# The S5 recurrence's scans with their powers and products in PSUM banks

## What is computed

```python
def s5_branch(u, A_re, A_im, log_dt, B_re, B_im, C_re, C_im, D, w_glu, b_glu):
    ...
    A_bar = jnp.exp(A * dt)
    B_bar = ((A_bar - 1.0) / A)[..., None] * Bc
    pows = jnp.exp(A[None] * dt[None] * steps)
    ...
    def step(h0, uc):
        bu = jnp.einsum('btgh,gnh->btgn', uc, B_bar)
        a = jnp.broadcast_to(A_bar, bu.shape)
        _, local = lax.associative_scan(combine, (a, bu), axis=1)
        states = local + pows * h0[:, None]
        y = jnp.einsum('btgn,ghn->btgh', states, Cc).real
        return states[:, -1], y
    ...
    y = ys.transpose(1, 0, 2, 3, 4).reshape(b, L, D_S5) + D.astype(f32) * uf
    y = jax.nn.gelu(y)
    y = y * jax.nn.sigmoid(y @ w_glu.astype(f32) + b_glu.astype(f32))
```

## Time and profile before

| | us |
|---|---|
| median of 3 runs | 4154.89 |
| lowest, highest run | 4148.94, 4157.69 |
| profiled execution | 4153.42 |
| its span (first to last instruction) | 4151.6 |
| TensorE busy | 3840.0 |
| VectorE busy | 2210.1 |
| GpSimd busy | 1041.6 |
| ScalarE busy | 902.8 |

### The profile page before, as it was taken

The page is one execution under the profiler, slowest core; times in us unless marked ns, Lnnn a source line. Parts: engine busy times, 40 slices in busy tenths (PEclk is TensorE's granted clock), DMA queues, the critical chain, the costliest instruction groups (busy, mean ns, idle before and its releaser), DMA issues.

```text
span 4151.6 us, 47406 instructions
## 1 busy us (share of the span) xinstructions
PE 3840.0 (92%) x19082; PEld 3102.2 (75%) x19082; DVE 2210.1 (53%) x2823; ACT 902.8 (22%) x1635; POOL 1041.6 (25%) x581
## 2 busy tenths in 40 slices
PE   6999998999999999999989998798999978889998
PEld 5677676788888887888866776577788767778777
DVE  5554557332323266999334523646254994653565
ACT  3434335200000032111010011302111012542131
POOL 1111111344444432333211211131322311003322
PEclk9999999999999999999999998898999986779999
DMA  2000000211212111222211212121553234222111
GB/s 88 21 26 23 29 26 16 71 66 56 66 56 66 63 43 36 87 86 81 71 51 36 71 42 76 44 64 46 138 117 79 81 87 122 62 60 81 61 51 61
DMA packets 139241, 260.25 MB, mean 63 GB/s; under 512 B 45632, under 2 KB 87616, under 8 KB 136000
## 3 DMA queue, kind: packets, MB, share of 16 engines
q1 hardware_dynamic: 72208, 156.26, 13.3%
q10 hardware_dynamic: 66864, 101.63, 7.2%
HBM read 209.35 MB, written 46.14 MB: 62 GB/s over the span
## 4 chain that ended last, share of the span: by engine, by line
PE 82%; DVE 12%; ACT 2%; issue 2%; DMA 1%; SPq 1%; POOL 1%; ACTq 0%; DVEq 0%; POOLq 0%
PE bank L572 22%; PE bank L574 22%; PE bank L573 22%; PE bank L784 2%; PE bank L954 2%; PE bank L821 1%; PE bank L691 1%; PE bank L804 1%; PE bank L943 1%; PE bank L1082 1%; DVE fb L1962 1%; DVE hn L1817 1%; DVE h L2315 1%; DVE xl L1828 1%; DVE ab L1965 1%
## 5 line engine op out<-in xcount | busy, mean ns | idle before, releaser
L572 PE MATMUL bank<-xh,wh 128*128 128x512 f32 x3008 | 1198.0, 398 | 75.1 <-DVE xl L1828 19.2
L573 PE MATMUL bank<-xl,wh 128*128 128x512 f32 x3008 | 1182.2, 393 | 0.0
L574 PE MATMUL bank<-xh,wl 128*128 128x512 f32 x3008 | 1180.9, 393 | 0.0
L529 POOL CAST wh<-raw 128x1024 fp32r<-128x1024 f32 x264 | 282.4, 1070 | 3004.9 <-PE bank L574 2951.3
L572 PEld LDWEIGHTS bank<-xh,wh 128*128 128x128 f32 x3008 | 571.4, 190 | 235.3 <-issue 38.3
L531 POOL TENSOR_TENSOR wl<-raw,wh 128x1024 fp32r<-128x1024 f32 x264 | 673.6, 2552 | 21.1
L574 PEld LDWEIGHTS bank<-xh,wl 128*128 128x128 f32 x3008 | 571.3, 190 | 121.4
L573 PEld LDWEIGHTS bank<-xl,wh 128*128 128x128 f32 x3008 | 572.3, 190 | 114.5
L2109 DVE SCALAR_TENSOR_TENSOR bank<-apad,cols,bank 128x512 f32<-128x512 f32 x406 | 267.9, 747 | 0.0
L1864 DVE TENSOR_TENSOR h<-bank,h 128x512 f32<-128x512 f32 x240 | 165.3, 690 | 153.3 <-PE bank L574 152.4
L1962 DVE TENSOR_TENSOR_SCAN fb<-fb 128x256 f32<-128x256 f32 (+7 forms) x128 | 189.5, 1521 | 73.6 <-ACT ab L1262 73.6
(11 more groups left out here) (340 smaller groups left out, 5408.1 us busy)
## 6 DMA issues: line engine op xcount, KB each, us to landing
raw<-in_wstream SPq DMA_DIRECT2D x264, 512.0 KB, 3.6
spills<-spill ACTq DMA_DIRECT2D x40, 512.0 KB, 2.7
rawm<-in_mod_w ACTq DMA_DIRECT2D x12, 1024.0 KB, 4.9
gate_spill<-gates ACTq DMA_DIRECT2D x16, 512.0 KB, 2.6
tabs<-in_rope ACTq DMA_DIRECT2D x4, 2048.0 KB, 8.5
f<-spills SPq DMA_DIRECT2D x8, 1024.0 KB, 5.7
h<-in_x ACTq DMA_DIRECT2D x4, 1024.0 KB, 11.8
tabs<-gate_spill ACTq DMA_DIRECT2D x4, 1024.0 KB, 7.0
```

Source lines behind the costliest of these rows:

```text
L529: nc.gpsimd.tensor_copy(wh[:, slot], raw[:, slot]).then_inc(S("panel_high"), 1)
L572: nc.tensor.matmul(o, lh, rh, start=start, stop=False)
L573: nc.tensor.matmul(o, lh, rl, start=False, stop=False)
L574: return nc.tensor.matmul(o, ll, rh, start=False, stop=stop)
```

## The change

The bank tensors 2 to 7 are declared after three tensors of two banks each, which are given up at once, so that `scan_a` lies over banks 2 and 3, `scan_t1` over 4 and 5, and `scan_t2` over 6 and 7. Before the first `within_run` one copy puts the powers `s5q` (1024 elements in each partition) into `scan_a`; `within_run` and `next_run` take their factors from there. The two temporaries of `advance` become `scan_t1` and `scan_t2`. So of the two tensors that each of its five operations reads, one lies in PSUM and one in `s5`; the two multiplications also write to PSUM. The order of the instructions is otherwise the same on all engines.

```diff
-        banks = [ctx.enter_context(nc.psum_tensor(f"bank{b}", [P, 512], F32)) for b in range(8)]
+        banks = [ctx.enter_context(nc.psum_tensor(f"bank{b}", [P, 512], F32)) for b in range(2)]
+        with ExitStack() as st:
+            scan_a, scan_t1, scan_t2 = [st.enter_context(nc.psum_tensor(f"scan{n}", [P, 2 * 512], F32)) for n in range(3)]
+        banks += [ctx.enter_context(nc.psum_tensor(f"bank{b}", [P, 512], F32)) for b in range(2, 8)]
...
-                pb_flat = pb[:, :, :, :, :].rearrange("p c q a h -> p (c q a h)")
-                s5t_flat = s5t[:, :, :, :, :].rearrange("p c q a h -> p (c q a h)")
+                powers_a = scan_a[:, :].rearrange("p (c q j) -> p c q j", c=2, q=S5_PAIRS)
 
                 def advance(new, old, a, shape):
                     size = 2 * S5_PAIRS * shape[-1]
                     t1, t2 = [t[:, 0:size].rearrange("p (c q n) -> p c q n", c=2, q=S5_PAIRS)
-                              for t in (pb_flat, s5t_flat)]
+                              for t in (scan_t1, scan_t2)]
                     link(TT(t1, a[0], old, ALU.mult))
                     link(TT(t2, a[1], old, ALU.mult))
...
                 def within_run(j):
                     shape = [P, 2, S5_PAIRS, S5_RUNS]
-                    a = [s5q[:, c, :, 0:1].unsqueeze(1).broadcast_to(shape) for c in range(2)]
+                    a = [powers_a[:, c, :, 0:1].unsqueeze(1).broadcast_to(shape) for c in range(2)]
...
                 def next_run(g):
                     shape = [P, 2, S5_PAIRS, S5_RUN]
-                    a = [s5q[:, c].unsqueeze(1).broadcast_to(shape) for c in range(2)]
+                    a = [powers_a[:, c].unsqueeze(1).broadcast_to(shape) for c in range(2)]
...
                 s5_local(KT - 1)
                 dve.wait_ge(S("s5_stored"), KT)
+                link(V.tensor_copy(powers_a, s5q[:, :, :, :]))
                 for j in range(1, S5_RUN):
                     within_run(j)
```

## The result

| | before | changed |
|---|---|---|
| median, us | 4152.68 (4 runs, 4148.94 to 4157.69) | 4125.02 (4 runs, 4122.91 to 4130.23) |
| profiled execution | 4153.42 | 4130.23 |
| its span | 4151.6 | 4128.2 |

The ratio is 0.9932, with an interval of 0.9916 to 0.9948: 28 us faster, between 22 and 35. A second comparison (experiment 1) gave 0.9936, interval 0.9923 to 0.9949. One of the six executions of the changed kernel there took 12841.23 us; it counts as slow and is left out of the ratio.

The account below looks back on a forecast made before the run. VectorE's queue before s5_outputs(0) was taken as the bound, keeping TensorE waiting. Hold-ups -27.9, copy +1.3 and two meetings +4.6 gave 22.0 us less: 4154.9 - 22.0 = 4132.9 us, range 4126 to 4145.

Parts of the forecast that it names:

- The bound: Before s5_outputs(0): VectorE's queue sets the end of both TensorE waits, 13.22 us for xc and 19.06 us for pb.
- The hold-ups: In the scan, operations beside GpSimd's cast and subtract of ten weight panels lose 27.9 us; a bank operand removes all.
- Own cost of a bank: In the scan's operations, reading or writing PSUM, also strided or over two banks, adds 0 us.
- (b): In the scan's multiplications, the powers' stride in the bank costs 10.3 us, giving 4143.2 us; chance 0.07.
- (d): In the scan, operations reading one bank and writing another, over two banks, run at half rate: 4172 us; chance 0.03.
- The copy: Ahead of the first within_run, copying 1024 elements into a bank adds 1.3 us to VectorE's queue.
- What comes back: Taps of tiles 6 and 7, still in SBUF, now run beside GpSimd's panel work: two meetings, 4.6 us lost.
- The sum: On VectorE's queue, 27.9 - 1.3 - 4.6 = 22.0 us earlier, all reaching the end of the kernel.
- The level and the range: Whole kernel: 4154.9 - 22.0 = 4132.9 us, range 4126 to 4145 with 2 us for scatter on either side.
- rival (a): The scan's strided part gets faster too, up to 21 us on the queue: 4132.3 us; chance 0.80 together with the forecast.
- (c): In the scan, operations with a bank are still held up by GpSimd; only the copy remains, 4156.2 us; chance 0.05.
- (e): The gain is given back after 3352 us, where something comes at its own time: 4150 us or so; chance 0.05.

Follow-up runs that it names:

- experiment 1: The changed kernel, unedited, timed again beside the kernel before: ratio 0.9936 (0.9923 to 0.9949); stretch from the last s5_local to the product's end 124.57 us.
- experiment 3: The changed kernel with only the powers in banks, both temporaries back in SBUF: ratio 0.9975 against the kernel before, stretch 138.48 us.
- experiment 4: The changed kernel with only the temporaries in banks, powers read from SBUF and no copy: ratio 0.9957 against the kernel before, stretch 134.05 us.
- experiment 6: GpSimd's subtract done twice for ten weight panels: ratio 1.0043 in the kernel before, 0.9940 in the changed kernel, both against the kernel before.
- experiment 2: The kernel before, unedited, profiled once more: stretch from the last s5_local to the product's end 149.56 us, rest of the program behind it 795.3 us.
- Experiment 7: The changed kernel with one more copy of the powers between next_run(5) and the taps of tile 7: stretch 126.49 us instead of 124.57, profiled only.
- experiment 8: The changed kernel with four-operation steps, two copies and next_run(4) placed earlier, taps of tiles 6 and 7 adding up in banks: 4122.58 us, ratio 0.9925.

## Why the prediction fell short

Its steps, in its own order:

- **The bound.** Right: TensorE waited for one queue of VectorE; the wait for `xc` went altogether and the second remained, 10.39 us instead of the 13 us forecast.
- **The hold-ups, -27.9 us.** Right as to cause (experiments 3, 4, 6) and nearly as to size. The scan's first part took 3293.30 - 3209.03 = 84.3 us, against 112.9 us before: -28.6 us. The 0.7 us more are small savings in each clean `within_run`, most of them in the strided multiplications: 1.03 us on average instead of 1.05 us. The powers' place alone doesn't explain it, since with one half of the tensors moved, either of them, they take 1.04 us (experiments 3 and 4).
- **Own cost of a bank, 0.** Right, and for the stride in part by luck: 0 had been chosen between a gain of 21 us and a cost of 10.3 us because no row showed the case. It holds for the stride and for the operations over two banks: 1.23 us for 1024 elements before and after. Rivals (b) and (d) fell with it. The 7.1 us that were estimated from the Trainium skill (VectorE: DVE Perf Modes, The TRN2 errata) didn't come; there the measurement decides.
- **The copy, +1.3 us.** Right: 1.22 us and the gap, 1.25 us. The wait for `xc` of tile 6, foreseen as a near miss, was 0.29 us.
- **What comes back, +4.6 us for two meetings.** This is the step that failed: the two together cost 2.1 us, 2.5 us less. The first one was there, with 6.77 us for the taps instead of 4.69 us. The second wasn't. The taps of tile 7 ran from 3310.82 to 3315.5, and GpSimd's cast came at 3314.64, when the last of them had begun. It had been counted because the two overlapped in time. What costs VectorE something is not the overlap but an operation that reads SBUF twice and is still to start; of these there was none left. The prediction's own times could have shown it: with the taps of tile 7 at 3308 their last one begins at about 3311.5, and the cast that they were to meet begins at 3311.42, so that at most one hold-up was left. Experiment 7 has such a case, and it cost 0.66 us.
- **The sum.** -28.6 + 1.25 + 0.3 + 2.1 = -25.0 us, the difference of the two stretches, where the forecast had -22.0. Of these 3.0 us the meetings are 2.5.
- **The level and the range.** The median of the changed kernel is 4132.9 - 4125.0 = 7.9 us below the forecast. The stretch explains 3.0 us of it. Another 2.2 us lie in the starting point: the forecast subtracts from 4154.89 us, the median of three runs, and with a fourth run the median before is 4152.68 us. The remaining 2.7 us, from 25 us to the 28 us of the medians, are scatter, as far as can be shown: the rest of the program moves by 4.3 us and its start by 1.1 us for one and the same kernel (experiment 2), and both comparisons hold 25 us in their intervals. The range allowed 2 us for that, although the three runs that it had before it lay 8.8 us apart; with the good end of its costs and 4 us it would have reached to 4124. That the rest of the program contributes nothing is shown within these 4 us, not better. The failed step moved the forecast, but not the good end of the range, which had left the meetings out.

Of rival (a), a faster strided part, 0.7 us are there; (c) is refuted by every maximum of the scan; (e) had no sign.

The Trainium skill (SBUF — State Buffer, Who interferes with whom) says that a VectorE instruction with two SBUF inputs contends with a GpSimd instruction that reads SBUF, and that issue order decides who blocks. The traces agree: 3.12 us for an operation of 1.04 us that came second, and 1.79 us for a cast of 1.04 us when it came second itself.

## What to carry to other kernels

When VectorE sets the end of a wait and GpSimd works beside it, look at the spread of one operation's durations before its mean: 1.1 and 3.2 us for the same shape is waiting, and moving one of its two read tensors to an idle PSUM bank takes it away. Do it for a whole chain of operations: with one half of the tensors moved, the other operations still waited for 13.1 or 9.9 us of the 27.9 us. And to price what is left, count the SBUF-only operations that still have to start while GpSimd runs, not the time in which they overlap.

## What was new about the hardware

- The hold-up goes by what is read: with the result in a bank but both inputs in SBUF an operation still took up to 2.93 us (experiment 4); with one input in a bank and the result in SBUF it stayed at 1.04 us (experiment 3). An operation with one tensor to read, from SBUF to SBUF, was held up too, 1.41 us instead of 0.81 us (experiment 3).
- A bank read in steps of 64 bytes, each element eight times, costs nothing beside an SBUF tensor with the same stride: 1.01 to 1.07 us for 512 elements, against 1.03 us and more from SBUF alone. Operations over two banks cost nothing either: 1.23 us for 1024 elements.
- A tap with one tensor to read loses time by a bank: 1024 elements take 0.81 us from SBUF to SBUF and 1.35 us from SBUF to a bank (experiment 8).
